# The expert matrix from rounded operands, more units of u beside it, and work for TensorE in two gaps

## What is computed

```
s = einsum('thpd,hpnd->thpn', q, sub_keys); sv, si = top_k(s, 16)
cand = sv[:, :, 0, :, None] + sv[:, :, 1, None, :]     # 8 heads, 16 x 16 pairs
top_v, top_i = top_k(cand, 16); g = softmax(top_v)
a = gelu(einsum('td,thkd->thk', x, u[experts]))
y = einsum('thk,thkd->td', g * a, v[experts])
```

## Time and profile before

| | us |
|---|---|
| median of 3 runs | 1410.67 (1408.16 to 1411.12) |
| the profiled execution's own time | 1407.76 |
| its span, first to last instruction | 1406.0 |
| mean granted TensorE clock | 0.996 of 2.4 GHz |
| PE, PEld, DVE, ACT, POOL busy | 1364.7, 1219.7, 984.8, 776.2, 353.3 |

### The profile page before, as it was taken

The page is one execution under the profiler, slowest core; times in us unless marked ns, Lnnn a source line. Parts: engine busy times, 40 slices in busy tenths (PEclk is TensorE's granted clock), DMA queues, the critical chain, the costliest instruction groups (busy, mean ns, idle before and its releaser), DMA issues.

```text
span 1406.0 us, 21411 instructions
## 1 busy us (share of the span) xinstructions
PE 1364.7 (97%) x8448; PEld 1219.7 (87%) x8448; DVE 984.8 (70%) x1677; ACT 776.2 (55%) x1265; POOL 353.3 (25%) x218
## 2 busy tenths in 40 slices
PE   6999999999999998999899999999999999999997
PEld 6898888999988777999899999888888888888886
DVE  5676686888868675799867664766666666676666
ACT  5455745444555454454499997444444454444443
POOL 1630000000034102898522231222222222222222
PEclk9999999999999999999999999999999999999999
DMA  7553246879777624467554545666566666655665
GB/s 240 163 161 106 76 169 237 282 261 327 271 256 277 250 87 153 143 223 220 172 154 146 156 142 170 206 202 205 195 211 216 215 206 208 210 195 197 216 216 194
DMA packets 190323, 278.81 MB, mean 198 GB/s; under 512 B 9184, under 2 KB 120544, under 8 KB 189968
## 3 DMA queue, kind: packets, MB, share of 16 engines
q1 hardware_dynamic: 184640, 266.19, 57.4%
q10 hardware_dynamic: 5184, 10.02, 1.9%
q0 software_dynamic: 400, 1.25, 0.3%
HBM read 266.41 MB, written 11.01 MB: 197 GB/s over the span
## 4 chain that ended last, share of the span: by engine, by line
PE 79%; DVE 11%; ACT 3%; DMA 3%; POOL 2%; issue 1%; DVEq 0%; SPq 0%; ACTq 0%; POOLq 0%
PE bank L706 18%; PE bank L644 14%; PE bank L711 9%; PE bank L671 8%; PE bank L649 7%; PE bank L617 6%; PE bank L676 4%; PE bank L990 4%; PE bank L621 3%; DMA sb_raw<-w_in 2%; PE bank L907 1%; ACT sb_hi L1024 1%; PE bank L926 1%; DVE sb_lo L1404 1%; POOL sb_lo L2014 1%
## 5 line engine op out<-in xcount | busy, mean ns | idle before, releaser
L1024 ACT ACTIVATE sb_hi<-sb_raw 128x1024 fp32r<-128x1024 f32 (+2 forms) x427 | 439.1, 1046 | 222.4 <-DMA sb_raw<-peer_v 50.8
L1404 DVE TENSOR_TENSOR sb_lo<-sb_raw,sb_hi 128x1024 fp32r<-128x1024 f32 (+2 forms) x312 | 424.6, 1377 | 179.9 <-ACT sb_hi L1024 178.1
L2014 POOL TENSOR_TENSOR sb_lo<-sb_raw,sb_hi 128x1024 fp32r<-128x1024 f32 x116 | 281.2, 2435 | 710.4 <-ACT sb_hi L1024 710.4
L644 PE MATMUL bank<-sb_act,sb_hi 128*128 128x256 f32 x2240 | 297.9, 286 | 1.3 <-DVE sb_act L1497 1.3
L644 PEld LDWEIGHTS bank<-sb_act,sb_hi 128*128 128x128 f32 x2240 | 280.2, 192 | 2.5 <-issue 1.3
L706 PE MATMUL bank<-sb_hi,sb_hid_hi 128*128 128x512 f32 x600 | 234.3, 391 | 0.2 <-ACT sb_hi L1024 0.2
L706 PE MATMUL bank<-sb_hi,sb_hid_lo 128*128 128x512 f32 x600 | 234.0, 390 | 0.0
L649 PE MATMUL bank<-sb_act,sb_lo 128*128 128x256 f32 x1120 | 157.9, 284 | 5.8 <-DVE sb_lo L1404 3.4
L711 PE MATMUL bank<-sb_lo,sb_hid_hi 128*128 128x512 f32 x600 | 161.1, 389 | 0.4 <-POOL sb_lo L2014 0.4
L649 PEld LDWEIGHTS bank<-sb_act,sb_lo 128*128 128x128 f32 x1120 | 144.7, 192 | 6.8 <-DVE sb_lo L1404 3.6
L711 PEld LDWEIGHTS bank<-sb_lo,sb_hid_hi 128*128 128x128 f32 x600 | 112.5, 188 | 24.1 <-POOL sb_lo L2014 0.8
(11 more groups left out here) (333 smaller groups left out, 1644.7 us busy)
## 6 DMA issues: line engine op xcount, KB each, us to landing
sb_raw<-peer_uT SPq DMA_DIRECT2D x128, 512.0 KB, 4.0
sb_raw<-peer_v SPq DMA_DIRECT2D x128, 512.0 KB, 4.8
sb_raw<-w_in SPq DMA_DIRECT2D x52, 512.0 KB, 4.6
sb_ada_w<-ada_wT SPq DMA_DIRECT2D x48, 512.0 KB, 5.6
sb_raw<-w_gate SPq DMA_DIRECT2D x22, 512.0 KB, 3.9
sb_raw<-w_up SPq DMA_DIRECT2D x22, 512.0 KB, 4.3
sb_raw<-w_down SPq DMA_DIRECT2D x22, 512.0 KB, 3.8
sb_raw<-w_out SPq DMA_DIRECT2D x16, 512.0 KB, 3.4
```

The source lines that it names most:

```text
L644: e.matmul(bank[:, j * T:(j + 1) * T], hi[:, k, j * P:(j + 1) * P], part[:, k0 + k, :], start=i == first_i and j == 0 and k == 0 and part ...
L1024: e.activation(flat_of(i, "hi"), flat_of(i, "raw"), ACT.Copy).then_inc(hi_done[i % R], 1)
L1404: e.tensor_tensor(flat_of(i, "lo"), flat_of(i, "raw"), flat_of(i, "hi").bitcast(F32), ALU.subtract).then_inc(lo_done[i % R], 1)
L2014: e.tensor_tensor(flat_of(i, "lo"), flat_of(i, "raw"), flat_of(i, "hi").bitcast(F32), ALU.subtract).then_inc(lo_done[i % R], 1)
```

## The change

- A token of G is one product with 256 moving columns, of rounded operands (fp32r): the first keys' one-hot matrix is the stationary side, and the moving side is the second keys' matrix times the rounded weights beside the same matrix times what rounding left. The sum of the two halves is G.
- A group is then: DVE compares (1024 elements), DVE multiplies the rounded weights into two tokens (256 elements), ACT into the other two (two instructions), DVE multiplies the rest into all four (512 elements), PE makes four products into two banks, ACT copies the first halves into G (two instructions of 256 elements), DVE adds the second halves (two of 256). Two one-hot buffers instead of three. Three banks serve u and four serve G.
- 36 units of u between the groups instead of 21, so 47 early and 17 late. Their lo parts are all made by POOL (early_G 1 instead of 2), and ACT makes hi one block ahead instead of three.
- UNIT_ORDER spreads the 17 late units: each is followed by two or three early ones.
- At the start PE makes 22 matmuls of 512 columns on zeros before the transposes; hi and lo of the first panel are made between the chunks, the lo of its first two blocks by POOL.
- Ahead of the norm of the feed-forward layer PE makes 14 matmuls of 128 and 7 of 512 columns whose result is not used.

```
-POOL_SHARE = dict(lat=0, d=0, uq=0, ukv=0, gate=0, b_mla=0, b_diff=0, w_out=0, early=-4, early_G=2, ctx_in2=1, w_gate=0, w_up=0, down=0, wq=1)
+POOL_SHARE = dict(lat=0, d=0, uq=0, ukv=0, gate=0, b_mla=0, b_diff=0, w_out=0, early=-4, early_G=1, ctx_in2=1, w_gate=0, w_up=0, down=0, wq=1)
...
-EARLY_BESIDE_G = 21
+EARLY_BESIDE_G = 36
...
-HOT_BUFS = 3
+HOT_BUFS = 2
+N_WARM, LO_FIRST = 22, 2
+N_FILL = 14
...
-G_LATER = 5
-TG = 4
+GELU_LATER = 4
+TG, TG_ACT, TG_BANK = 4, 2, 2
 N_G = T // TG
 G_FROM = 4
 V_LAG = HID_BUFS - 1
-UNIT_ORDER = [v for e in range(EARLY) for v in (EARLY + e, e)] + list(range(2 * EARLY, N_UNITS))
+N_LATE = N_UNITS - EARLY
+UNIT_ORDER = [v for k in range(N_LATE) for v in (EARLY + k, *range(k * EARLY // N_LATE, (k + 1) * EARLY // N_LATE))]
...
-                lo_on_pool[i] = share != 0 and (n_split % share == 0 if share > 0 else n_split % -share != 0)
+                lo_on_pool[i] = i < LO_FIRST or share != 0 and (n_split % share == 0 if share > 0 else n_split % -share != 0)
...
+            bank = take("warm")
+            pe.wait_ge(*warm_set.at())
+            for i in range(N_WARM):
+                ins = e.matmul(bank[:, :], warm[:, 0:P], warm, start=True, stop=True)
+            ins.then_inc(*fills("warm"))
+            give("warm")
...
+            bank, rounded = take("fill"), merged_T.hi
+            for i in range(N_FILL):
+                e.matmul(bank[:, 0:P], rounded[:, 0, 0:P], rounded[:, 1, 0:P], start=True, stop=True)
+            for i in range(N_FILL // 2):
+                ins = e.matmul(bank[:, :].rearrange("p (c t) -> p c t", c=2), rounded[:, 0, 0:P], rounded[:, 2:4, :], start=True, stop=True)
+                if i >= N_FILL // 2 - 2:
+                    ins.then_inc(*(fills("fill") if i == N_FILL // 2 - 2 else gives("fill")))
+            give("fill")
...
+            u_banks, G_banks = idle_banks[0:3], idle_banks[3:7]
...
-                    bank, h = take("G", n), hot[n % HOT_BUFS]
-                    pe.wait_ge(*hot_done.at(n))
-                    for j in range(TG):
-                        ins = e.matmul(bank[:, j * P:(j + 1) * P], h[:, 1, j, :], h[:, 0, j, :], start=True, stop=True)
-                    ins.then_inc(*fills("G", n))
-                    give("G", n)
+                    h = hot[n % HOT_BUFS]
+                    for j0 in range(0, TG, TG_BANK):
+                        bank = take("G", n, j0, among=G_banks)
+                        pe.wait_ge(*hot_done.at(n))
+                        for j in range(TG_BANK):
+                            ins = e.matmul(bank[:, j * T:(j + 1) * T], h[:, j0 + j, 0, :], h[:, j0 + j, 1:3, :], start=j == 0, stop=j == TG_BANK - 1, skip_group_check=True)
+                        ins.then_inc(*fills("G", n, j0))
+                        give("G", n, j0)
...
-            hi_first()
-            norm_out("x", col("norm_mix_g", 0, 8), None, [(cols_in, 16)])
+            for c2 in range(DC // 2):
+                norm_out("x", col("norm_mix_g", 0, 8), None, [(cols_in, 16)], range(c2, c2 + 1))
+                if c2 < DC // 2 - 1:
+                    hi_until(("lat", 0), c2, 0)
...
+            def G_rounded(q):
+                if q == 0:
+                    for b in range(3):
+                        act.wait_ge(early_stored[b], 16 * len(range(b, EARLY_BESIDE_SELECT, 3)))
+                    act.wait_ge(x_parked, 16)
+                    act.wait_ge(g2_parked, 16)
+                    act.wait_ge(*freed("picks", 1))
+                for j0 in range(0, TG, TG_BANK):
+                    t0 = q * TG + j0
+                    act.wait_ge(*full("G", q, j0))
+                    e.activation(Gv[:, :, t0:t0 + TG_BANK], psum("G", q, j0)[:, :].rearrange("p (t w i) -> p w i t", t=TG_BANK, w=2)[:, 0], ACT.Copy).then_inc(*G_hi.inc(q, j0))
...
-                    hi_until(("uT", order[at][1]), order[at][2])
+                    hi_until(("uT", order[at][1]), order[at][2], 1)
                 elif at < len(order) and order[at][0] == "G":
                     q = order[at][1]
+                    if q >= HOT_BUFS:
+                        G_rounded(q - HOT_BUFS)
                     act.wait_ge(*hot_eq.at(q))
-                    for j in range(TG):
-                        h = hot[q % HOT_BUFS][:, 1, j, :]
-                        ins = e.activation(h, h, ACT.Copy, scale=pT[:, 2, q * TG + j:q * TG + j + 1])
-                    ins.then_inc(*hot_done.inc(q))
-                if at >= G_LATER:
-                    what, n, b = order[at - G_LATER]
-                    if what == "G":
-                        if n == 0:
-                            for b in range(3):
-                                act.wait_ge(early_stored[b], 16 * len(range(b, EARLY_BESIDE_SELECT, 3)))
-                            act.wait_ge(x_parked, 16)
-                            act.wait_ge(g2_parked, 16)
-                            act.wait_ge(*freed("picks", 1))
-                        copy_out(Gv[:, :, n * TG:(n + 1) * TG], psum("G", n)[:, :].rearrange("p (t i) -> p i t", t=TG), "G", n)
-                    elif b == 1:
+                    for j in range(TG_ACT):
+                        h = hot[q % HOT_BUFS][:, j]
+                        ins = e.activation(h[:, 1, :], h[:, 2, :].bitcast(F32), ACT.Copy, scale=w_hi[:, q * TG + j:q * TG + j + 1].bitcast(F32))
+                    ins.then_inc(*hot_hi.inc(q))
...
+            e.memset(warm.bitcast(F32), 0).then_inc(*warm_set.inc())
...
+            dve.wait_ge(*full("warm"))
+            e.memset(red, 0).then_inc(*gives("warm"))
+            norm_lo("x", col("norm_mix_g", 0, 8), chunks=range(0, 3))
+            lo_until(("lat", 0), 2, 0)
+            norm_lo("x", col("norm_mix_g", 0, 8), chunks=range(3, 4))
...
+            def hot_equal(q):
+                h = hot[q % HOT_BUFS]
+                if q >= HOT_BUFS:
+                    dve.wait_ge(*full("G", q - HOT_BUFS, TG - TG_BANK))
+                toks = slice(q * TG, (q + 1) * TG)
+                e.tensor_tensor(h[:, :, 0:3:2, :].rearrange("p t w n -> p w t n"), iota_p.unsqueeze(1).unsqueeze(1).to_broadcast([P, 2, TG, P]),
+                                pT[:, 0:2, toks].unsqueeze(3).to_broadcast([P, 2, TG, P]), ALU.is_equal).then_inc(*hot_eq.inc(q))
+                dve.wait_ge(*hot_eq.at(q))
+                e.tensor_tensor(h[:, TG_ACT:TG, 1, :], h[:, TG_ACT:TG, 2, :].bitcast(F32), w_hi_row[:, q, :].unsqueeze(2).to_broadcast([P, TG - TG_ACT, P]), ALU.mult).then_inc(*dve_self.inc())
+            def hot_left(q):
+                rows = hot[q % HOT_BUFS][:, :, 2, :]
+                dve.wait_ge(*dve_self.at())
+                dve.wait_ge(*hot_hi.at(q))
+                e.tensor_tensor(rows, rows.bitcast(F32), w_lo_row[:, q * TG:(q + 1) * TG].unsqueeze(2).to_broadcast([P, TG, P]), ALU.mult).then_inc(*hot_done.inc(q))
+            def G_sum(q):
+                for j0 in range(0, TG, TG_BANK):
+                    v = Gv[:, :, q * TG + j0:q * TG + j0 + TG_BANK]
+                    dve.wait_ge(*G_hi.at(q, j0))
+                    e.tensor_tensor(v, psum("G", q, j0)[:, :].rearrange("p (t w i) -> p w i t", t=TG_BANK, w=2)[:, 1], v, ALU.add).then_inc(*gives("G", q, j0))
...
+                        c, bank = slice(t * P, (t + 1) * P), psum("picks", t)
+                        dve.wait_ge(*full("picks", t))
+                        e.tensor_copy(pT[:, 0:2, c], bank[:, 0:2 * P].rearrange("p (w t) -> p w t", w=2))
+                        own(e.tensor_copy(w_hi[:, c], bank[:, 2 * P:3 * P]))
+                        e.tensor_tensor(w_lo_row[:, c], bank[:, 2 * P:3 * P], w_hi[:, c].bitcast(F32), ALU.subtract).then_inc(*gives("picks", t))
...
+                    own(e.tensor_copy(w_hi_row, w_hi.bitcast(F32).rearrange("p (q j) -> p q j", j=TG)[:, :, TG_ACT:TG]))
...
+                    hot_equal(n)
...
+                        G_sum(n - HOT_BUFS)
+                    hot_left(n)
+            for q in range(N_G - HOT_BUFS, N_G):
+                G_sum(q)
...
+            lo_until(("lat", 0), LO_FIRST - 1, 0)
```

More of the change, by code:

```diff
@@ L576, in tensor_program, with take @@
             pe = Waits(e)
-            def take(*key):
-                b = idle_banks.pop(0)
+            def take(*key, among=range(8)):
+                b = next(b for b in idle_banks if b in among)
+                idle_banks.remove(b)
                 use_of[key] = (b, n_used[b])
```

43 lines of the change are left out of this document (22 added, 21 removed).

## The result

The changed kernel takes 1392.3 us (median of 4 runs, 1390.68 to 1393.54); the kernel before, run beside it, 1409.41 us (1407.91 to 1411.12). The ratio is 0.9876, interval 0.9863 to 0.989: 17.1 us faster. 1388 was forecast, with 1383 to 1394 as the likeliest case's own range. The profiled execution takes 1391.79 us (span 1390.0), so its span is 16.0 us shorter than before; the sum of the prediction was -21.3. The case foreseen came about, and 5.3 us of the gain are missing in the profiled execution (4.2 by the medians).

The account below looks back on a forecast made before the run. TensorE was taken to bound the G and last stages; the terms -26.7 + 3.0 + 4.5 + 1.5 - 2.6 - 1.0 sum to -21.3 us, giving 1386.5 to 1389.4, forecast 1388 us, likeliest range 1383 to 1394.

Parts of the forecast that it names:

- Products of G: G stage: 256 single rounded products at 0.119 us each replace 57.3 us of the chain with 30.6, -26.7 us.
- 15 units moved: From last stage to G stage: each unit costs 5.74 us early against 5.54 late, +3.0 us.
- TensorE stays the bound: G stage: TensorE needs 3.53 us per group, VectorE 3.17, and the others also stay under 237 us, 0.
- A2: G stage: mild hand-over limit, a period of 3.65 to 3.8 us per group, +8 to +17 us; chance 0.08.
- A: G stage: hand-over between engines paid in series, 4.1 us per group, +37 us, 1425 us; chance 0.06.
- D: G stage: GpSimd blocks VectorE on a group's last product, a period of 4.05 us, +34, 1422 us; chance 0.03.
- Contention of GpSimd and VectorE: G stage: new VectorE operations each have one operand in a bank, so GpSimd's lo parts do not block them, 0.
- The seam: G stage to last stage: v's first product waits for hid lo, +4.5 us (0 to 7), then slow clock, +1.5.
- The last stage otherwise: Last stage: the ring's rate stays and loads at 220 GB/s keep up, 0, upper end +17 us.
- Rival B: Last stage: parked loads come late and starve it, 0.36 us for each of 47, +17 us, 1405 us; chance 0.10.
- The start: Kernel start: hi and lo made between chunks end the first panel about 19.2 us, -2.6 us (0 to -4).
- the fill: Ahead of the feed-forward norm: 21 unused matmuls keep TensorE's clock up, -1.0 us (-1.8 to +1.3).

Follow-up runs that it names:

- e5: Changed kernel with every product of G issued twice with the same operands: 1421.86 us.
- e4: Changed kernel with 21 units of u in the G stage instead of 36: 1426.71 us.
- e3: Changed kernel with VectorE making every second lo part of the first two units of the G stage: 1388.01 us.
- e1: Changed kernel with the second late unit of u one place forward, so the last stage begins late, early, late: 1386.92 us.
- e6: Changed kernel with one warm-up matmul on zeros at the start instead of 22: 1394.21 us.
- e7: Changed kernel with 4 and 2 filling matmuls ahead of the feed-forward norm instead of 14 and 7: 1391.36 us.
- e2: Changed kernel with ACT copying G's last two groups ahead of the last parked gelus instead of behind them: 1391.92 us.
- e9: Changed kernel with the edits of e1, e2 and e3 together: 1380.91 us.
- e10: Changed kernel with the edits of e1 and e3 together, without that of e2: 1382.70 us.
- e11: Changed kernel with 29 units of u in the G stage instead of 36, plus the edits of e2 and e3: 1382.64 us.

## Why the prediction was right, and where it lost 5 us

*Products of G, -26.7.* Right: 0.120 us each (e5).

*15 units moved, +3.0, and the stage of G.* Together with the products +59.4 was forecast. Measured is 61.1 less the new wait of 3.2 at its end, 57.9, so the sum was 1.5 too high. The stage before took 166.0 us, where the prediction's own terms give 64 x 0.895 + 37 x 2.87 = 163.5; of the 2.5 between them 1.5 are short waits of TensorE between groups, which the sum left out and the change removed. After, the terms give 222.9 and the stage took 223.9. With the five blocks ahead of the first product (14.4 us) that is 223.9 + 14.4 = 238 us on TensorE, where 236 to 240 was forecast.

*TensorE stays the bound, at 0.* Right, and the slack was larger than thought: 2.9 us for a group on VectorE instead of 3.17 (e4). The rivals A2, A and D did not come: no instruction of a group shows GpSimd's 2.4 us (line 1984 takes 1.22 to 1.23 us, line 1994 0.67 to 0.69, line 2001 0.43 to 0.51, in all cases), although GpSimd was busy 158.7 of 229 us.

*Contention of GpSimd and VectorE, at 0.* This step failed in its reasoning, as the seam's did below. It was read for the instructions of the group alone. The same parts that move to GpSimd also cover the end of the selection, where VectorE has small instructions with two SBUF inputs. The rule that I used to set the term to 0 was the one that priced it. It cost 2.8 us up to the first product, and e3, which takes it away, gives 4.3 (3.7 at the first product in the trace).

*The seam, +4.5 and +1.5.* The wait of v was there (4.1) and e1 shows its price with the clock, 4.7 to 5.4. The other wait, 3.2 us and a slower first unit (1.5), was missing, and it is the largest error of the sum: the prediction followed hid, not the bank that G's last sums hold. Its upper end of 7 named late sums of G but not where they wait, behind ACT's last gelu. The sum over both is 3.2 + 1.5 + 4.1 + 1.5 = 10.4 before rounding, instead of 6.0. The part of the clock is that of this one execution (see e3).

*The last stage otherwise, 0.* Rival B did not come. From v's first to its last instruction TensorE is busy without a gap:

```profile
941.00:1379.00 438.00, 438.00 (x2044) 367.17 (x2045) 284.62 (x310) 208.77 (x236) 96.06 (x40) 1.00 0.66 218
```

The load was forecast at 220 GB/s and is 218. (The prediction's 7.4 us between parked loads should read 443/47 = 9.4; nothing was worked out from it.) Without the seam's 7.2 us the stretch shrinks by 85.1 instead of 83.1. The traces give most of the 2.0 us between them. The 32 late units before take 178.1 us, 5.57 each and not 5.54, so 15 of them are 83.5. And v's products before have 1.3 us of short waits and slow instructions in them that the changed kernel does not have, most of it at two places:

```profile
890.81 1.20 PE L711 MATMUL bank<-sb_lo,sb_hid_hi 128*128 128x512 f32 x4 [0.36 <-POOL sb_lo L2014]
...
1235.47 0.50 PE L706 MATMUL bank<-sb_hi,sb_hid_hi 128*128 128x512 f32 x1 [0.20 <-ACT sb_hi L1024]
```

*The start, -2.6, and the fill, -1.0.* The first as forecast (-2.5 here, -2.0 to -2.5 over the traces), though e6 gives somewhat under half of it to the warm clock; of the second 0.5 came at its place, and e7 shows nothing in the time.

*The end.* From v's last instruction to the end it takes 10.6 us instead of 9.3. The chain of waits runs through a load here, not through TensorE. VectorE's first final sum, after and before:

```profile
1377.63 0.70 DVE L2055 TENSOR_TENSOR bank<-bank,sb_slot 128x512 f32<-128x512 f32 x1 [4.07 <-DMA sb_slot<-parked_g]
```

```profile
1393.62 0.70 DVE L1984 TENSOR_TENSOR bank<-bank,sb_slot 128x512 f32<-128x512 f32 x1 [3.18 <-PE bank L711]
```

The load is issued when TensorE frees its slot, and takes 5.5 us to land, 3.7 before. It does not come from the change: e2, e6 and e7 have the same last stage as the changed kernel, do not wait for this load, and end 9.3 us after v's last instruction, while e3 and e9 wait for it and take 10.7 and 10.3. What makes the load slow in some executions stays open.

The deviations are +0.3 (start and fill), +2.8, -1.5, +4.4 (seam), -2.0 and +1.3, together the missing 5.3 us. The first cause, the seam, and the second, the blocked selection, are shown by e1, e2, e3 and by their sum in e9. There is some luck in the figure: the two errors of mechanism are 7.2 us, and the small terms that ran the other way (-1.5 and -2.0) took half of it back.

## What to carry to other kernels

When work moves to GpSimd, look at every VectorE instruction that it will now run beside, not only at those of the stage that the move is for: short ones with two SBUF inputs each cost one whole GpSimd instruction, and a serial chain of them pays every time. At a seam list everything that the first unit of the next stage needs, its banks too, and find the last gelu or copy in whose shadow each stands; two waits there hide one another, so an edit that gives nothing alone may give its gain once the next one is covered (e10 against e9, where e2 alone gave nothing). When two engines are balanced over groups, count only the work that stands between the groups: five blocks ahead of the first one made level engines look like 6% of slack, and ten places without a block cost 2.7 us and ate the gain (e11). And compare traces mark by mark: a wait for one load at the end differed by 1.3 us between executions of the same last stage.
